# Attention queries written twice by GpSimd and turned once per head, in a two-layer diffusion trunk

## The chip, the cores and the metric

The kernel runs on one core of one Trainium2 chip. The metric is the device time of one execution in microseconds (us), the median of the runs. A core has TensorE (PE: matrix products and transposes; PEld is its weight load), VectorE (DVE), ScalarE (ACT), GpSimd (POOL) and SyncE (SP, which issues DMAs). Engines run side by side and wait for each other by semaphores. SBUF is the memory that all of them read; PSUM holds TensorE's results, in eight banks of 512 float32 per partition.

## The reference

Two trunk layers run over 1024 latent and 128 context tokens of width 1024. Each is modulated norm, mixer, then a mixture of experts. The change touches the attention of both mixers only. There, with queries and keys normalised and rotated:

```python
# layer 0: 8 query heads, 2 key/value heads, head width 64
s = jnp.einsum('bqkgd,bskd->bkgqs', qblk, k) * scale
pr = jax.nn.softmax(s, axis=-1)
return jnp.einsum('bkgqs,bskd->bqkgd', pr, v)

# layer 1: differential attention, 8 heads, two maps each, value width 128
s = jnp.einsum('bqphd,bsphd->bphqs', qblk, k) * scale
pr = jax.nn.softmax(s, axis=-1)
w = pr[:, 0] - lam * pr[:, 1]
return jnp.einsum('bhqs,bshe->bqhe', w, v)
```

All is float32. A float32 number x is used in TensorE's faster format as high part (x rounded to it) and low part (x less the high part), and a product is summed from the parts.

## The kernel before, in words

`attention` runs once per layer, in 2 groups of heads in layer 0 and 4 in layer 1; a group has 4 query maps (`nq`). In a group, the first part projects nine token tiles of 128 (`project`, t = 0 to 8), rotates and scales them on VectorE (`begin`, `finish_tile`) and leaves the queries in `qtok`. The second part runs over units (`unit_0`, `unit_1`). A unit is one query tile with one head: 4 units per tile in layer 0, 2 in layer 1, where a unit has two maps. One step of the unit loop issues, in TensorE's order, the scores of the next unit, transposes of the probabilities of an earlier one (`turn_probs`) and the product with the values of one still earlier (`values`).

Scores need the queries turned, with head width on the partitions. The contraction is 128 deep for a width of 64, since both halves of the partitions are used: the keys `ks` have their high part in one half and their low part in the other, and `qst` has for each map a first operand (v = 0) and a second (v = 1).

Before the change this is made so. For tile `qt`, VectorE (`split_queries`) writes the high part, the low part and the high part again into `qq`, three instructions of 128x256. TensorE (`stage_half`, L1271) turns it in two halves, each with four transposes of 128x128 into one bank; the windows [high, low] and [low, high] of `qq` give v = 0 and v = 1. ScalarE copies each bank into `qst` (L1398).

The order of the work is written out by hand: `program` and `unit_0`/`unit_1` are walked by TensorE and ScalarE, and VectorE has its own loop. All turns (keys, queries, probabilities) and the output of `values` share two PSUM banks in alternation. `next_bank` lets TensorE write a bank only when the reader of the use two places earlier is done: for a turn ScalarE's copy (`turn_read`), for an output VectorE's read (`o_read`). The scores use the other six banks, two sets of three in turn; VectorE takes their row maximum (`maxima`, L1691), ScalarE the exponential (L1467), and VectorE scales or mixes them (`mix`; L1703 in layer 0, L1709 in layer 1). L1310 are the transposes of the probabilities, L1327 and L1339 the products with the values.

GpSimd computes in this stage only inverse roots for the norms (L1150; in layer 1 L1154 and L1156 too).

## Time and profile before

| | us |
|---|---|
| median of 3 runs | 3293.04 (3290.2 to 3293.2) |
| span of the profiled execution | 3285.2 |
| PE, DVE, ACT, POOL busy in it | 3111.3, 2259.3, 1887.4, 618.3 |
| attention of layer 0, about | 225 to 595 |
| attention of layer 1, about | 1570 to 2358 |

The profile gives the span from the first to the last instruction; the run time of the profiled execution itself is not listed beside it. The median of the runs lies 7.8 us over the span. Part 2 of the page divides the span into 40 slices of 82 us, in tenths of busy time; attention is slices 3 to 7 and 20 to 28:

```profile
PE   6999989989999999997999999999997999999999
DVE  4777677557766666765686776867747666766666
PEclk9999999999999999998999999999998999999999
```

### The profile page before, as it was taken

How to read it: one execution, taken by the hardware profiler on the slowest of the kernel's cores; microseconds unless marked ns; L12 is line 12 of the kernel's file. 1: busy time of each engine (PE TensorE's matmuls, PEld its weight loads, DVE VectorE, ACT ScalarE, POOL GpSimd, SP SyncE). 2: the span in 40 equal slices, each digit the busy share in tenths (PEclk: the TensorE clock that was granted, in tenths of full speed). 3: DMA queues.
4: the chain of work that ended last, by engine and by line, in shares of the span. 5: the costliest groups of instructions: out<-in, count | busy, mean ns of one | idle time of the engine just before them, and what ended most of it. 6: DMA issues, size and time to landing. Idle time of an engine off the chain costs nothing. (4 is left out here: it accounts for less than half of the span.)

```text
span 3285.2 us, 55861 instructions
## 1 busy us (share of the span) xinstructions
PE 3111.3 (95%) x20268; PEld 2409.3 (73%) x20268; DVE 2259.3 (69%) x2853; ACT 1887.4 (57%) x2679; POOL 618.3 (19%) x479
## 2 busy tenths in 40 slices
PE   6999989989999999997999999999997999999999
PEld 4767878865777676765887888888885676767776
DVE  4777677557766666765686776867747666766666
ACT  3556848425665666554375583846723666556564
POOL 1200010001223322222111111021100222232221
PEclk9999999999999999998999999999998999999999
DMA  7230000449888888877010100100145888888885
GB/s 236 87 132 21 1 23 1 155 170 377 293 303 286 296 299 298 287 252 233 7 43 8 42 8 9 36 8 23 52 161 220 294 300 299 287 284 309 291 297 154
DMA packets 214175, 565.42 MB, mean 172 GB/s; under 512 B 33699, under 2 KB 71272, under 8 KB 213736
## 3 DMA queue, kind: packets, MB, share of 16 engines
q1 hardware_dynamic: 203614, 529.21, 44.6%
q0 software_dynamic: 9472, 33.57, 4.2%
q8 instruction: 111, 1.82, 0.2%
q14 instruction: 72, 0.59, 0.1%
q10 hardware_dynamic: 906, 0.23, 0.0%
HBM read 524.00 MB, written 38.94 MB: 171 GB/s over the span
## 5 line engine op out<-in xcount | busy, mean ns | idle before, releaser
L2188 DVE TENSOR_TENSOR moe_lo<-moe_raw,moeg_hi 128x2048 fp32r<-128x2048 f32 x384 | 882.8, 2327 | 289.3 <-ACT moeg_hi L2185 153.9
L2185 ACT CAST moeg_hi<-moe_raw 128x2048 fp32r<-128x2048 f32 x384 | 729.0, 1911 | 439.4 <-PE psum L2591 320.9
L1170 PE MATMUL psum<-attn_w_hi,attn_hs 128*128 128x512 f32 (+2 forms) x1424 | 368.3, 342 | 15.8 <-DVE attn_hs L1558 10.6
L1691 DVE TENSOR_REDUCE attn_neg_max<-psum 128x1 f32<-128x1280 f32 (+1 forms) x216 | 292.6, 1354 | 80.0 <-PE psum L1297 77.0
L1297 PE MATMUL psum<-attn_ks,attn_qst 128*128 128x512 f32 (+2 forms) x1200 | 310.7, 376 | 21.6 <-ACT attn_e L1467 19.5
L1467 ACT ACTIVATE attn_e<-psum,attn_neg_max 128x1280 f32<-128x1280 f32 (+1 forms) x216 | 264.6, 1226 | 60.9 <-DVE attn_neg_max L1691 54.8
L1170 PEld LDWEIGHTS psum<-attn_w_hi,attn_hs 128*128 128x128 f32 x1424 | 249.1, 189 | 47.8 <-DVE attn_hs L1558 11.8
L2591 PE MATMUL psum<-moe_lo,moeh_x_hi 128*128 128x512 f32 x960 | 262.0, 395 | 0.0
L2591 PE MATMUL psum<-moeg_hi,moeh_x_hi 128*128 128x512 f32 x960 | 261.6, 394 | 0.0
L2591 PE MATMUL psum<-moeg_hi,moeh_x_lo 128*128 128x512 f32 x960 | 260.6, 393 | 0.0
L1170 PE MATMUL psum<-attn_w_lo,attn_hs 128*128 128x256 f32 (+2 forms) x712 | 240.1, 337 | 0.0
L1297 PEld LDWEIGHTS psum<-attn_ks,attn_qst 128*128 128x128 f32 x1200 | 200.2, 190 | 51.3 <-ACT attn_e L1467 21.2
L2176 PE MATMUL psum<-moe_raw,moeh_xc 128*32 128x512 f32 x2048 | 236.2, 602 | 0.6 <-DMA moe_raw<-in_l_w_up 0.6
L2591 PEld LDWEIGHTS psum<-moeg_hi,moeh_x_hi 128*128 128x128 f32 x960 | 177.8, 188 | 51.1 <-issue 14.0
L1398 ACT COPY attn_pt<-psum 128x512 f32<-128x512 f32 (+2 forms) x400 | 191.7, 505 | 37.8 <-PE psum L1310 29.7
L2591 PEld LDWEIGHTS psum<-moeg_hi,moeh_x_lo 128*128 128x128 f32 x960 | 180.3, 188 | 42.1
L1310 PE MATMUL psum<-ident,attn_e 128*128 128x128 f32 x1296 | 197.4, 278 | 14.5 <-ACT attn_pt L1398 8.2
L2591 PEld LDWEIGHTS psum<-moe_lo,moeh_x_hi 128*128 128x128 f32 x960 | 180.5, 188 | 41.0
L1150 POOL TENSOR_TENSOR rstd<-ssq,neg_half 128x8 f32<-128x8 f32 (+1 forms) x54 | 80.0, 1482 | 548.6 <-DVE ssq L1590 548.6
L1310 PEld LDWEIGHTS psum<-ident,attn_e 128*128 128x128 f32 x1296 | 144.4, 141 | 48.0 <-issue 24.5
L2169 POOL COPY moeh_xc<-moe_x_ctx 128x64 f32 (+1 forms) x64 | 127.9, 2029 | 215.4 <-PE psum L2176 190.4
L1339 PE MATMUL psum<-attn_v,attn_pt 128*128 128x128 f32 x1296 | 158.3, 277 | 5.7 <-ACT attn_pt L1398 3.8
(360 smaller groups left out, 5389.7 us busy)
## 6 DMA issues: line engine op xcount, KB each, us to landing
moe_raw<-in_l_w_gate SPq DMA_DIRECT2D x256, 512.0 KB, 4.1
moe_raw<-in_l_w_up SPq DMA_DIRECT2D x256, 512.0 KB, 5.1
moe_raw<-in_l_w_down SPq DMA_DIRECT2D x128, 1024.0 KB, 6.1
ada_w<-in_l_ada_w SPq DMA_DIRECT2D x19, 1024.0 KB, 13.9
ada1h_w<-in_l_ada_w SPq DMA_DIRECT2D x9, 1024.0 KB, 10.7
lru_ada<-in_l_ada_w SPq DMA_DIRECT2D x8, 1024.0 KB, 7.7
lru_late<-in_l_ada_w SPq DMA_DIRECT2D x8, 1024.0 KB, 11.8
out_w<-in_l_w_out SPq DMA_DIRECT2D x16, 512.0 KB, 5.9
```

The costliest lines, as they stand in the source:

```text
L1170: last = pe.matmul(out, hs[t % 2][:, part, k, :], right, start=(i == 0 and n == 0), stop=(i == KB - 1 and n == 2))
L1297: last = pe.matmul(m.psum[:, into:into + step], qst[(u // per_tile) % 2][:, qm, v, :], ks[:, km, col:col + step], start=(v == 0), stop=(v ...
L1310: last = pe.transpose(m.psum[:, at + (i - b) * P:at + (i - b + 1) * P], src[:, i * P:(i + 1) * P], m.ident[:, :])
L1339: last = pe.matmul(m.psum[:, at:at + dv], pt[u % 2][:, i * P:(i + 1) * P], vt[:, kt, col:col + dv], start=(i == 0), stop=(i == len(tiles) ...
L1398: act.copy(out, src).then_inc(s["turn_read"], 1)
L1467: act.activation(out[:, 0:hi - lo], m.psum[:, score_at(n):score_at(n) + hi - lo], ACT.Exp, bias=neg_max[:, n:n + 1], accum_out=sums[:, n:n ...
L1691: dve.tensor_reduce(neg_max[:, n:n + 1], m.psum[:, score_at(n):score_at(n) + hi - lo], AX.X, ALU.max, negate=True).then_inc(s["maxed"], 1)
L2169: last = pool.tensor_copy(dst[:, :, j, :], mm.x_ctx[:, :, ds(e * 8 + j * P, 8)])
L2176: last = pe.matmul(m.psum[32 * g:32 * g + 32, 6 * BANK:7 * BANK], mm.xc[:, k, :], mm.raw[k][:, g // 2, (g % 2) * BANK:(g % 2 + 1) * BANK], ...
L2185: act.copy(mm.hi[slot % 4][:, :, :], mm.raw[slot][:, :, :]).then_inc(mm.s["hi_ready"], 1)
L2188: dve.tensor_tensor(mm.lo[slot][:, :, :], mm.raw[slot][:, :, :], mm.hi[slot % 4][:, :, :].bitcast(F32), ALU.subtract).then_inc(mm.s["lo_re ...
L2591: last = pe.matmul(m.psum[:, at:at + BANK], x[:, k, :], w[:, j, half * BANK:(half + 1) * BANK], start=(k == 0 and i == 0), stop=(k == KB - ...
```

## The change

GpSimd now writes each query tile twice over into `q_twice`, unsplit. TensorE turns it once per map, four transposes into one bank in place of eight into two, and the result lies on both halves of the partitions. ScalarE casts the bank into the first operand (high part, one copy of 128x512), and VectorE subtracts that from the bank to give the second operand (low part, 128x512). The bank is free after VectorE's subtraction (`q_low`).

```diff
+            def write_twice(j, qt):
+                wait_value(m, pool, s["k_split"], j * turns_k + (qt + PT_TILES + 1))
+                wait_value(m, pool, s["q_turned"], j * NT + qt)
+                view = qtok[:, qt, :].rearrange("p (n d) -> p n d", d=HD)
+                pool.tensor_copy(q_twice[:, :, :, :], view.unsqueeze(2).broadcast_to([P, nq, 2, HD])).then_inc(s["q_twice"], 1)
...
+                    if t in (3, 6):
+                        write_twice(j, (3, 6).index(t))
+                for u in range(units + OUT_LAG):
+                    if u % per_tile == 0 and u // per_tile + 2 < NT:
+                        write_twice(j, u // per_tile + 2)
+                    if l == 1 and u >= OUT_LAG:
+                        normal_of_out(j, u - OUT_LAG)
...
+                        elif what == "queries":
+                            pe.wait_ge(s["q_low"], j * NT + count)
...
-                def stage_half(qt, half):
...
+                def stage(qt):
+                    pe.wait_ge(s["q_twice"], j * NT + (qt + 1))
+                    at = next_bank(queries=qt)
+                    for i in range(nq):
+                        last = pe.transpose(m.psum[:, at + i * P:at + (i + 1) * P],
+                                            q_twice[:, i, :, :].rearrange("p v d -> p (v d)"), m.ident[:, :])
+                    last.then_inc(s["q_turned"], 1)
...
+                    act.wait_ge(s["q_turned"], j * NT + (qt + 1))
+                    act.copy(qst[qt % 2][:, 0, :, :], m.psum[:, at:at + nq * P].rearrange("p (n t) -> p n t", t=P)
+                             ).then_inc(s["q_high"], 1)
...
-                def split_queries(qt):
...
+                def subtract_high(qt):
+                    at = query_bank[qt]
+                    dve.wait_ge(s["q_high"], j * NT + (qt + 1))
+                    dve.tensor_tensor(qst[qt % 2][:, 1, :, :], m.psum[:, at:at + nq * P].rearrange("p (n t) -> p n t", t=P),
+                                      qst[qt % 2][:, 0, :, :].bitcast(F32), ALU.subtract).then_inc(s["q_low"], 1)
...
+    def stage_after(u):
+
+        qt = u // per_tile + (1, 2)[l]
+        return qt if u % per_tile == 1 and qt >= 2 and qt < NT else None
```

The orders also move. Tiles 2 to 8 are turned inside a unit step (`stage_after`): in layer 0 where both halves stood before, between the second and the third piece of the scores; in layer 1 in one odd step, where the halves stood in two steps. VectorE subtracts after the row maximum in layer 0, and after `mix` and before the second row maximum in layer 1. Tile 0's subtraction stands behind `project(4)`, tile 1's behind the first row maxima.

In the lists below, each name in `waits` is that of a semaphore's first use in the program; semaphores are used again under other names, and the text says which is meant. Lines after the change are L1284 (query turn), L1305 (scores), L1318 (turn of probabilities), L1347 (values), L1648 (subtraction), L1688 (row maximum).

TensorE in a step of layer 0 with a query turn, before:

```order
L1271 MATMUL psum<-ident,attn_qq 128x128 [waits ada0_8_row_read,ada0_8_turned]
L1271 MATMUL psum<-ident,attn_qq 128x128 x3
L1297 MATMUL psum<-attn_ks,attn_qst_2086 128x256 x2
L1271 MATMUL psum<-ident,attn_qq 128x128 [waits ada0_8_row_read]
L1271 MATMUL psum<-ident,attn_qq 128x128 x3
L1310 MATMUL psum<-ident,attn_e_2080 128x128 [waits ada0_8_row_read,lru_pad_zeroed]
L1310 MATMUL psum<-ident,attn_e_2080 128x128 x3
L1310 MATMUL psum<-ident,attn_e_2080 128x128 [waits ada0_8_row_read]
L1310 MATMUL psum<-ident,attn_e_2080 128x128 x3
L1297 MATMUL psum<-attn_ks,attn_qst_2086 128x512 [waits lru_gates_zeroed]
```

and now, where the last wait (printed `lru_gates_zeroed`) is for `q_low`:

```order
L1284 MATMUL psum<-ident,attn_q_twice 128x128 [waits ada0_8_row_read,ada0_8_turned]
L1284 MATMUL psum<-ident,attn_q_twice 128x128 x3
L1305 MATMUL psum<-attn_ks,attn_qst_2086 128x256 x2
L1318 MATMUL psum<-ident,attn_e_2080 128x128 [waits ada0_8_row_read,lru_h_split]
L1318 MATMUL psum<-ident,attn_e_2080 128x128 x3
L1318 MATMUL psum<-ident,attn_e_2080 128x128 [waits lru_gates_zeroed]
L1318 MATMUL psum<-ident,attn_e_2080 128x128 x3
L1305 MATMUL psum<-attn_ks,attn_qst_2086 128x512 [waits lru_h_high]
```

Four transposes and one bank are gone, and the second bank of the next turn of probabilities waits for VectorE in place of ScalarE.

VectorE around a query tile in layer 0, before:

```order
L1691 TENSOR_REDUCE attn_neg_max<-psum 128x1 [waits ada0_8_folded]
L1643 CAST attn_qq<-attn_qtok 128x4x64 [waits ada0_8_used]
L1644 CAST attn_qq<-attn_qtok 128x4x64
L1646 TENSOR_TENSOR attn_qq<-attn_qtok,attn_qq 128x4x64
L1691 TENSOR_REDUCE attn_neg_max<-psum 128x1 [waits ada0_8_folded]
L1698 RECIPROCAL attn_inv<-attn_sums 128x1 [waits lru_gates_zeroed]
L1703 TENSOR_SCALAR attn_e_2080<-attn_e_2080,attn_inv 128x1280
```

and now, from the reduction that reads the scores of the same step:

```order
L1688 TENSOR_REDUCE attn_neg_max<-psum 128x1 [waits lru_pad_zeroed]
L1648 TENSOR_TENSOR attn_qst_2085<-psum,attn_qst_2085 128x512 [waits lru_gates_loaded]
L1688 TENSOR_REDUCE attn_neg_max<-psum 128x1 [waits lru_pad_zeroed]
L1695 RECIPROCAL attn_inv<-attn_sums 128x1 [waits lru_h_high]
L1700 TENSOR_SCALAR attn_e_2079<-attn_e_2079,attn_inv 128x1280
```

The three small instructions are gone from another step, and the subtraction stands behind the row maximum.

TensorE in a step of layer 1 with (half) a query turn, before:

```order
L1271 MATMUL psum<-ident,attn_qq 128x128 [waits lru_gelu_square]
L1271 MATMUL psum<-ident,attn_qq 128x128 x3
L1297 MATMUL psum<-attn_ks,attn_qst_11285 128x512 x2
L1297 MATMUL psum<-attn_ks,attn_qst_11285 128x256 x2
L1215 REGISTER_ALU [waits o0_scored]
L1310 MATMUL psum<-ident,attn_e_11279 128x128 [waits lru_gelu_square]
L1310 MATMUL psum<-ident,attn_e_11279 128x128
L1215 REGISTER_ALU [waits lru_gelu_square]
L1339 MATMUL psum<-attn_v,attn_pt_11281 128x128 [waits lru_gelu_square]
L1339 MATMUL psum<-attn_v,attn_pt_11281 128x128 x9
```

and now, where L1347 waits (printed `lru_last_ready`) for `q_low`:

```order
L1284 MATMUL psum<-ident,attn_q_twice 128x128 [waits lru_gelu_square]
L1284 MATMUL psum<-ident,attn_q_twice 128x128 x3
L1305 MATMUL psum<-attn_ks,attn_qst_11173 128x512 x2
L1305 MATMUL psum<-attn_ks,attn_qst_11173 128x256 x2
L1231 REGISTER_ALU [waits o0_soft]
L1318 MATMUL psum<-ident,attn_e_11167 128x128 [waits lru_gelu_square]
L1318 MATMUL psum<-ident,attn_e_11167 128x128
L1322 MATMUL psum<-ident,attn_o_11191 128x128 [waits o0_parted]
L1347 MATMUL psum<-attn_v,attn_pt_11170 128x128 [waits lru_last_ready,lru_gelu_square]
L1347 MATMUL psum<-attn_v,attn_pt_11170 128x128 x9
```

The product with the values is the use two places behind the turn, and its bank now waits for VectorE.

VectorE in a step of layer 1, before:

```order
L1691 TENSOR_REDUCE attn_neg_max<-psum 128x1 [waits lru_gelu_tanh]
L1698 RECIPROCAL attn_inv<-attn_sums 128x2 [waits lru_last_ready]
L1705 TENSOR_SCALAR attn_ratio<-attn_sums,attn_inv,neg_lambda 128x1
L1709 SCALAR_TENSOR_TENSOR attn_e_11279<-attn_e_11280,attn_ratio,attn_e_11279 128x1280
L1690 REGISTER_ALU
L1691 TENSOR_REDUCE attn_neg_max<-psum 128x1 [waits lru_gelu_tanh]
L1641 REGISTER_ALU
L1643 CAST attn_qq<-attn_qtok 128x4x64 [waits lru_root_ready]
L1644 CAST attn_qq<-attn_qtok 128x4x64
L1646 TENSOR_TENSOR attn_qq<-attn_qtok,attn_qq 128x4x64
```

and now:

```order
L1688 TENSOR_REDUCE attn_neg_max<-psum 128x1 [waits o0_scored]
L1695 RECIPROCAL attn_inv<-attn_sums 128x2 [waits o0_expd]
L1702 TENSOR_SCALAR attn_ratio<-attn_sums,attn_inv,neg_lambda 128x1
L1706 SCALAR_TENSOR_TENSOR attn_e_11167<-attn_e_11168,attn_ratio,attn_e_11167 128x1280
L1648 TENSOR_TENSOR attn_qst_11173<-psum,attn_qst_11173 128x512 [waits lru_rec_done]
L1687 REGISTER_ALU
L1688 TENSOR_REDUCE attn_neg_max<-psum 128x1 [waits o0_scored]
```

The subtraction stands between the mix (L1706, before L1709) and the second row maximum.

## Rows read from the trace of the kernel before

**Rows 1.** Busy time in windows; window, length, busy (count) of each engine, PEclk, DMA.
```profile
225.00:270.00 45.00, 38.96 (x213) 35.90 (x214) 37.59 (x102) 15.96 (x36) 8.19 (x7) 1.00 0.02 4
...
300.00:400.00 100.00, 97.88 (x964) 82.18 (x964) 72.83 (x112) 80.53 (x142) 0.00 (x0) 1.00 0.01 1
...
1880.00:1930.00 50.00, 50.00 (x380) 46.19 (x380) 44.16 (x62) 44.83 (x99) 6.42 (x16) 1.00 0.00 1
```

**Rows 2.** Groups of instructions; count | busy us, mean ns | idle before.
```profile
L1271 PE MATMUL psum<-ident,attn_qq 128*128 128x128 f32 x432 | 65.3, 276 | 3.5 <-ACT attn_pt L1398 1.9 <-ACT attn_ks L1398 1.5
...
L1646 DVE TENSOR_TENSOR attn_qq<-attn_qtok,attn_qq 128x256 f32<-128x256 f32 x54 | 23.0, 425 | 5.1 <-issue 1.3
```

**Rows 3.** Windows of two units of layer 0, with and without a query turn.
```profile
309.87:318.31 8.44, 8.35 (x82) 7.00 (x80) 5.18 (x8) 6.91 (x13) 0.00 (x0) 1.00 0.00 0
318.31:325.55 7.24, 7.24 (x75) 6.15 (x73) 6.00 (x11) 5.68 (x11) 0.00 (x0) 1.00 0.01 2
```

**Rows 4.** Timeline of layer 0; start us, us, engine, instruction, [idle before <-releaser].
```profile
312.06 0.60 PE L1271 MATMUL psum<-ident,attn_qq 128*128 128x128 f32 x4
...
312.42 0.49 PE L1297 MATMUL psum<-attn_ks,attn_qst 128*128 128x256 f32 x2
...
312.70 1.26 ACT L1398 CAST attn_qst<-psum 128x512 fp32r<-128x512 f32 x2 [0.53 <-PE psum L1271]
...
312.94 1.49 DVE L1691 TENSOR_REDUCE attn_neg_max<-psum 128x1 f32<-128x1280 f32 x1 [1.20 <-PE psum L1297]
...
313.43 1.24 PE L1310 MATMUL psum<-ident,attn_e 128*128 128x128 f32 x8
...
314.43 0.71 PE L1297 MATMUL psum<-attn_ks,attn_qst 128*128 128x512 f32 x2
```

**Rows 5.** Timeline of layer 0 near 280 us, VectorE to TensorE.
```profile
279.83 0.89 DVE L1703 TENSOR_SCALAR attn_e<-attn_e,attn_inv 128x1280 f32<-128x1280 f32 x1
...
280.78 1.09 PE L1310 MATMUL psum<-ident,attn_e 128*128 128x128 f32 x8 [0.19 <-DVE attn_e L1703]
```

**Rows 6.** Single lines; count: duration ns min/median/max, first and last start, shapes.
```profile
L1600 DVE TENSOR_TENSOR attn_zb<-psum,attnw_sin x64: 410/414/416, 1575.6 to 2235.5; 128x256 f32<-128x256 f32 x64
...
L2783 DVE TENSOR_TENSOR moeh_hid_lo<-psum,moeh_hid_hi x30: 1223/1224/1225, 821.0 to 3225.0; 128x1024 fp32r<-128x1024 f32 x30
...
L2481 POOL CAST moeh_x_hi<-moeh_x_tmp x30: 1041/1041/1496, 791.9 to 3207.4; 128x1024 fp32r<-128x1024 f32 x30
...
L2169 POOL COPY moeh_xc<-moe_x_ctx x64: 233/2295/2332, 766.5 to 3182.8; 128x64 f32 x48, 128x64 f32<-128x64 f32 x16
```

**Rows 7.** Timeline of layer 1, from 1888 us.
```profile
1888.75 1.04 PE L1310 MATMUL psum<-ident,attn_e 128*128 128x128 f32 x8
...
1890.09 0.60 PE L1271 MATMUL psum<-ident,attn_qq 128*128 128x128 f32 x4
...
1890.45 0.95 PE L1297 MATMUL psum<-attn_ks,attn_qst 128*128 128x512 f32 x4
...
1890.94 1.55 DVE L1709 SCALAR_TENSOR_TENSOR attn_e<-attn_e,attn_ratio,attn_e 128x1280 f32<-128x1280 f32 x1
...
1891.56 2.40 PE L1339 MATMUL psum<-attn_v,attn_pt 128*128 128x128 f32 x20
...
1892.41 1.48 DVE L1691 TENSOR_REDUCE attn_neg_max<-psum 128x1 f32<-128x1280 f32 x1
...
1894.95 1.17 PE L1310 MATMUL psum<-ident,attn_e 128*128 128x128 f32 x8
```

**Rows 8.** Timeline of layer 1, opening of a group.
```profile
1859.10 0.73 PE L1297 MATMUL psum<-attn_ks,attn_qst 128*128 128x512 f32 x2 [1.15 <-ACT attn_e L1467]
```

**Rows 9.** Timeline of an experts' stage: GpSimd and VectorE.
```profile
987.00 2.38 POOL L2483 TENSOR_TENSOR moeh_x_lo<-moeh_x_tmp,moeh_x_hi 128x1024 fp32r<-128x1024 f32 x1 [0.32 <-issue]
...
988.88 4.85 DVE L2188 TENSOR_TENSOR moe_lo<-moe_raw,moeg_hi 128x2048 fp32r<-128x2048 f32 x2 [3.31 <-PE psum L2176]
...
996.06 4.48 DVE L2188 TENSOR_TENSOR moe_lo<-moe_raw,moeg_hi 128x2048 fp32r<-128x2048 f32 x2
```

More of the change, by code:

```diff
@@ L937, in attention @@
     qst_at = put.pos[0]
-    qst = [put(f"qst{i}", [P, nq, 2, P], F32R) for i in range(2)]
-    qq = put("qq", [P, nq, 3, HD])
+    qst = [put(f"qst{i}", [P, 2, nq, P], F32R) for i in range(2)]
+    q_twice = put("q_twice", [P, nq, 2, HD])
+    put("spare", [P, nq, HD])
     khl_at = put.pos[0]
@@ L1022, in unit_1 @@
             make["scores"](u + 1, 1, 0)
-        if half_after(u) is not None:
-            make["stage_half"](*half_after(u))
+        if stage_after(u) is not None:
+            make["stage"](stage_after(u))
         if u >= 1:
@@ L1200, in group, with next_bank @@
                 turn, uses, keys_at = [0], [], {}
-                def next_bank(output=None, last=None):
+                def next_bank(output=None, last=None, queries=None):
                     n = len(uses)
@@ L1217, in next_bank @@
                         uses.append(("last", last))
+                    elif queries is not None:
+                        uses.append(("queries", queries + 1))
                     else:
@@ L1260, in last_v @@
                     pe.sem_inc(s["w_used"], 1)
-                staged = {}
-                def stage_half(qt, half):
-                    if half == 0:
-                        pe.wait_ge(s["q_split"], j * NT + (qt + 1))
-                    at = next_turn()
-                    for i in range(2):
-                        flat = qq[:, 2 * half + i, :, :].rearrange("p v d -> p (v d)")
-                        for v in range(2):
-                            last = pe.transpose(m.psum[:, at + (2 * i + v) * P:at + (2 * i + v + 1) * P],
-                                                flat[:, v * HD:v * HD + P], m.ident[:, :])
-                    last.then_inc(s["turned"], 1)
-                    staged[qt, half] = turn[0]
-                def stage(qt):
-                    for half in range(2):
-                        stage_half(qt, half)
+                def stage(qt):
+                    pe.wait_ge(s["q_twice"], j * NT + (qt + 1))
[4 more added lines that the diff above has]
+                    last.then_inc(s["q_turned"], 1)
                 def scores(u, which, piece=None):
@@ L1283, in scores @@
                     if piece in (None, 0):
-                        if u % per_tile == 0:
-                            pe.wait_ge(s["turn_read"], j * TURNS + staged[u // per_tile, (1, which)[l]])
+                        if u % per_tile == 0 and which == 0:
+                            pe.wait_ge(s["q_low"], j * NT + (u // per_tile + 1))
                         if u == 0 and which == 0:
@@ L1663, in count_last, with count_stage @@
                         used[0] += 1
-                def count_half(qt, half):
-                    count[0] += 1
+                def count_stage(qt):
+                    query_bank[qt] = turn_bank(used[0])
                     used[0] += 1
-                    staged_at[qt] = count[0]
-                def count_stage(qt):
-                    for half in range(2):
-                        count_half(qt, half)
                 def count_probs(u, part):
@@ L1683, in group @@
                 program(dict(cache_keys=count_cache, project=none, last_z=count_last, last_v=count_last, turn_keys=count_keys,
-                             stage=count_stage, stage_half=count_half, scores=none, exps=none, turn_probs=count_probs, values=count_values, ahead=none), last_group)
+                             stage=count_stage, scores=none, exps=none, turn_probs=count_probs, values=count_values, ahead=none), last_group)
                 def maxima(u, which):
```

66 lines of the change are left out of this document (25 added, 41 removed).

## The prediction

> **What bounds the kernel now.** I read the busy time in windows first, because the change touches only the attention stages. The reader is to see that the kernel has two kinds of stretch there [rows 1]. In the projection of layer 0 (225 to 270 us) TensorE is busy 38.96 of 45 us and VectorE 37.59, so VectorE sets the pace. In the unit loops TensorE is busy 97.88 of 100 us in layer 0 and all of 50.00 us in layer 1. There, an instruction taken off TensorE shortens the kernel, and any new wait of TensorE lengthens it. VectorE is at 73% in the unit loop of layer 0 and at 88% in that of layer 1, so it isn't the bound, but it works in order, and what stands in its queue ahead of a signal decides when the signal comes.
>
> Second, the groups of instructions: TensorE turns queries 432 times, 65.3 us busy, and VectorE's subtraction for them runs 54 times at 425 ns [rows 2]; 54 is 9 tiles times 6 groups. Third, the timelines of one step of each layer, which carry the sum.
>
> **TensorE's saving.** 216 of the 432 transposes go. Four of them occupy TensorE for 0.36 us when they flow: the query turn starts at 1890.09 and the next product at 1890.45 [rows 7]. The 0.60 us of the row holds the tail of the pipeline, which overlaps. In layer 0 the turn costs more: a pair of units with it takes 8.44 us and one without it 7.24 [rows 3], so 1.20 for eight transposes, of which 0.72 is work and 0.48 waits for ScalarE's casts of the two banks.
>
> **The new wait.** Before, the bank of a query turn was free when ScalarE had copied it. Now it is free when VectorE has subtracted, and VectorE comes to that only after what stands before it in its own list. In both layers TensorE wants that bank again two uses later. The orders of the instructions say which instruction that is: in layer 0 the second bank of the next turn of probabilities, in layer 1 the product with the values. Behind it stands everything else of TensorE, and so the next scores, their maxima and exponentials.
>
> Layer 0, tiles 2 to 8. The third piece of the scores is issued at 312.42, and the row maximum starts after it at 312.94, after 1.20 us of idleness, and takes 1.49 [rows 4]. Neither changes, since four transposes still stand ahead of that piece. VectorE starts an instruction some 0.08 us before the one ahead ends (mix from 1890.94 for 1.55, next at 1892.41) [rows 7]. So the subtraction starts at 314.35; ScalarE's cast, which starts at 312.70 [rows 4], is over long before. Its duration isn't in the trace in this shape. The nearest rows are a product with a PSUM operand of 128x256 at 0.41 and a subtraction from PSUM of 128x1024 at 1.22 [rows 6]; between them by width, 128x512 takes 0.68, which I use, with 0.41 and 1.22 as ends. TensorE starts 0.06 after a signal of VectorE (279.83 + 0.89 = 280.72, start 280.78) [rows 5]. That gives 314.35 + 0.68 + 0.06 = 315.09, and 0.36 for the four transposes: 315.45 for the next scores, which start at 314.43 now [rows 4]. Net +1.02 us per tile, the saved transposes included. There are 7 tiles in 2 groups: 14 x 1.02 = +14.3 us. Nothing takes it back, as TensorE has next to no idle time in the loop.
>
> Layer 1, tiles 2 to 8. In the odd step four transposes remain, so nothing is saved there. The mix runs from 1890.94, the next place in VectorE's list is at 1892.41, and there the subtraction goes: it ends at 1893.09, TensorE goes on at 1893.15. It wants to start the values at 1891.56 [rows 7]. Stall 1.59 us. In the even step the other half goes, 0.36, and with VectorE's three small instructions gone the turn of probabilities takes 1.04 in place of 1.17, since it waited there for the output's read behind them [rows 7]: 0.13 more. Net 1.59 - 0.36 - 0.13 = +1.10 us per tile. Tiles 3 to 8 in 4 groups: 24 x 1.10 = +26.4 us. The second row maximum comes 0.6 later in VectorE's list, but its scores' exponential isn't wanted before TensorE's next step, which is itself 1.59 later.
>
> Tile 1 and 2 of layer 1 are staged in the opening of the unit loop, where TensorE waits for exponentials (1.15 us at 1859.10) [rows 8], so VectorE's order counts directly: two subtractions of 0.68 come in, and three small instructions, at most 3 x 0.425 = 1.28 [rows 2], go. That is between 0 and 0.7; I take 0.4, 4 x 0.4 = +1.6 us. Tile 0 of layer 1 is turned while TensorE sets the pace: -0.36 x 4 = -1.4 us. Tiles 0 and 1 in layer 0: VectorE loses its small instructions and gets a subtraction, in its own stretch; within 0.6 us per group either way, taken as nothing.
>
> **GpSimd and ScalarE.** GpSimd is idle in the unit loop of layer 0 and busy 6.42 of 50 us in that of layer 1 [rows 1]. It now makes 54 copies of 128x512. A cast of 128x1024 takes 1.04 and a copy of 128x64 0.23 at best [rows 6]; by width between them 0.6. Each copy starts when the tile before has been turned and is wanted two to four steps later, some 12 us in layer 1 and 16 in layer 0, so even 2.38, the slowest row of 128x1024 [rows 9], costs TensorE nothing. ScalarE has one cast less per tile; in the unit loop it is off the path, worth nothing. The clock: TensorE was granted 1.00 (2.4 GHz) also in the stretch where it was 87% busy [rows 1], so I charge nothing for stalls of 1.6 us.
>
> **The sum.** 14.3 + 26.4 + 1.6 - 1.4 = +40.9 us on the span of 3285.2, so 3326.1; the median of the runs lies 7.8 above the span, so 3293.04 + 40.9 = 3334. If the subtraction took 0.41, 42 tiles would give 11 less; at 1.22, 23 more.
>
> **Rival 1, the bank is free in time (faster).** If VectorE's subtraction were done before TensorE wants the bank, only the saving would stand: layer 0 14 x (1.20 - 0.36) = 11.8, layer 1 28 x 0.49 = 13.7, tile 0 1.4, together -27: 3266 us. It decides at 1891.56 in layer 1. In layer 0 the turn of probabilities starts at 313.43 [rows 4] and would start up to 0.7 earlier (0.36 of work, the rest waits), its second bank 0.36 later: between 313.1 and 313.8. For it: VectorE is idle 1.20 us ahead of the row maximum in layer 0. Against it: its list has the maximum first, and that waits for a later product.
>
> **Rival 2, GpSimd holds VectorE up.** The trace shows that the two exclude each other: a 128x64 copy takes 0.23 at best and 2.30 in the median [rows 6], and where GpSimd's subtraction runs until 989.38, VectorE's two from 988.88 take 4.85 in place of 4.48 [rows 9]. If each copy in layer 1 met the mix and held it for 0.6, the stall would grow by that: 28 x 0.6 = 17, so 3351. Against it: in layer 1 the copy stands behind GpSimd's roots, after the mix, while VectorE reads PSUM. In layer 0 the scaling isn't on the way to the bank.
>
> The Trainium skill, page "SBUF — State Buffer", section "SBUF: two separate sides", says the same more sharply: GpSimd and a VectorE instruction with two SBUF inputs or in a two-port mode share one pair of ports, and whichever starts first keeps it for the whole instruction. The 4.85 us agree. By that rule a subtraction with one operand in PSUM would not be blocked, the mix would.
>
> **Rival 3, half of the stall is made up.** While TensorE waits, VectorE and ScalarE catch up, and small waits behind go. Layer 0 has 2.1 us of TensorE's idle time in 100 [rows 1], layer 1 none, so it would need turns of probabilities that wait without being seen. Half of the sum: +20, 3313.
>
> **How the numbers follow.** Forecast 0.74, with a range of its own of 3322 to 3350; rival 2 0.10; rival 3 0.08; rival 1 0.06; that it all cancels 0.02. The range of 8 in 10 goes from 3314 to 3353: below by the short subtraction and part of rival 3, above by rival 2 and a longer subtraction. A difference of 0.2% (6.6 us) is about what can be told from none. Faster 0.06, same 0.02, slower 0.92.
>
> **What would show it.** In the profile after: L1318 in layer 0 and L1347 in layer 1 idle ahead of them for 1.3 to 2.0 and for 1.6 us, released by L1648, 14 and some 24 to 28 times, together near 65 us; a pair of units with a turn in layer 0 at 9.5 us; two units of layer 1 at 13.5 in place of 12.4 (2 x 6.2, from 1888.75 to 1894.95 [rows 7]); L1648 at 0.68 us; GpSimd's copy at 0.6. The prediction is wrong if those waits are not there, if VectorE subtracts before the maximum ends, or if the mix (L1706) is longer than 1.55 or starts late with GpSimd busy.

## The result, and the profile after

| | before | after |
|---|---|---|
| median of 4 runs, us | 3291.62 | 3349.51 |
| lowest to highest, us | 3289.72 to 3293.2 | 3347.78 to 3350.99 |
| profiled execution: time, us | not listed | 3347.78 |
| profiled execution: span, us | 3285.2 | 3345.8 |
| granted clock of the profiled execution, mean | 0.988 | 0.982 |

The ratio is 1.0174, with a 95% interval of 1.016 to 1.0189. The kernel became 57.9 us slower; 40.9 were forecast, with a range of 3314 to 3353 that holds the result. The span grew by 60.6 us. The profiled execution of the kernel before is one of its shorter ones: its spans on record beside the experiments go from 3285.2 to 3297.2 us. So what is read from the two traces lies some 3 us above the loss of the medians.

Windows of the changed kernel, as [rows 1]: window, length, busy time (count) of TensorE matmuls, weight loads, VectorE, ScalarE and GpSimd, then the granted clock. The first lies in layer 0's unit loop, the second in layer 1's. The third is the opening of the unit loop of layer 1's second group, where the granted clock is 0.56.

```profile
300.00:400.00 100.00, 90.40 (x888) 76.35 (x888) 66.41 (x93) 72.82 (x128) 3.08 (x5) 1.00 0.01 1
1910.00:1960.00 50.00, 45.30 (x328) 40.28 (x327) 40.46 (x48) 39.11 (x87) 7.27 (x19) 1.00 0.00 1
...
1885.00:1892.00 7.00, 5.98 (x25) 4.97 (x24) 6.15 (x8) 3.76 (x6) 0.62 (x1) 0.56 1.03 296
```

TensorE, which was busy 97.88 of 100 us and all of 50, now stands idle for 9.6% and 9.4% of the first two. That is most of the loss; VectorE and ScalarE became less busy too, so neither is the new bound.

Whom TensorE waits for, in layer 0's stage, then in layer 1's; columns: us in total, times, the longest.

```profile
PE psum L1318 <- DVE attn_qst L1648: 24.4, 14, 1.7
PE psum L1184 <- DVE attn_hs L1565: 7.4, 10, 1.0
```

```profile
PE psum L1347 <- DVE attn_qst L1648: 35.6, 24, 3.6
PE psum L1305 <- ACT attn_e L1474: 15.1, 13, 2.6
```

L1648 is VectorE's subtraction. The two lines foretold, L1318 (the second bank of the next turned probabilities) and L1347 (the values), wait for it 14 and 24 times, 60 us together. L1339, which is L1347 in the kernel before, waited for VectorE 1.7 us in all of layer 1 before.

The timeline of one step of layer 0, the answer to [rows 4]: start us, us, engine, instruction, idle time before it and what ended it.

```profile
314.49 0.60 PE L1284 MATMUL psum<-ident,attn_q_twice 128*128 128x128 f32 x4
314.85 0.49 PE L1305 MATMUL psum<-attn_ks,attn_qst 128*128 128x256 f32 x2
315.13 0.59 ACT L1461 CAST attn_qst<-psum 128x512 fp32r<-128x512 f32 x1 [0.53 <-PE psum L1284]
315.17 0.60 PE L1318 MATMUL psum<-ident,attn_e 128*128 128x128 f32 x4
...
315.37 1.49 DVE L1688 TENSOR_REDUCE attn_neg_max<-psum 128x1 f32<-128x1280 f32 x1 [1.20 <-PE psum L1305]
...
316.78 0.68 DVE L1648 TENSOR_TENSOR attn_qst<-psum,attn_qst 128x512 fp32r<-128x512 f32 x1
317.52 0.66 PE L1318 MATMUL psum<-ident,attn_e 128*128 128x128 f32 x4 [1.75 <-DVE attn_qst L1648]
317.93 0.71 PE L1305 MATMUL psum<-attn_ks,attn_qst 128*128 128x512 f32 x2
```

It reads as the working had it: the maximum, then the subtraction, then 0.06 us, then TensorE, which had been ready for 1.75 us. ScalarE's cast was over at 315.72, a microsecond before VectorE came to it.

One odd step of layer 1, the answer to [rows 7]:

```profile
1913.01 1.33 ACT L1474 ACTIVATE attn_e<-psum,attn_neg_max 128x1280 f32<-128x1280 f32 x1 [0.87 <-DVE attn_neg_max L1688]
1913.60 1.03 PE L1318 MATMUL psum<-ident,attn_e 128*128 128x128 f32 x8
...
1914.48 0.73 PE L1305 MATMUL psum<-attn_ks,attn_qst 128*128 128x512 f32 x2
1914.62 1.06 ACT L1406 COPY attn_pt<-psum 128x512 f32<-128x512 f32 x2
...
1915.25 0.66 PE L1284 MATMUL psum<-ident,attn_q_twice 128*128 128x128 f32 x4
...
1915.79 1.55 DVE L1706 SCALAR_TENSOR_TENSOR attn_e<-attn_e,attn_ratio,attn_e 128x1280 f32<-128x1280 f32 x1
...
1917.26 0.68 DVE L1648 TENSOR_TENSOR attn_qst<-psum,attn_qst 128x512 fp32r<-128x512 f32 x1
1917.86 1.48 DVE L1688 TENSOR_REDUCE attn_neg_max<-psum 128x1 f32<-128x1280 f32 x1
1918.09 2.13 PE L1347 MATMUL psum<-attn_v,attn_pt 128*128 128x128 f32 x17 [1.15 <-DVE attn_qst L1648]
```

The values start 2.84 us after the turn of the queries; before, 1.47 (1890.09 to 1891.56). The pieces of the two kernels in windows of two units, as [rows 3]: layer 0 with a query turn, without, and layer 1.

```profile
312.29:321.82 9.53, 7.79 (x79) 6.61 (x77) 5.79 (x9) 6.37 (x12) 0.62 (x1) 1.00 0.00 0
321.82:329.05 7.23, 7.23 (x74) 6.13 (x72) 5.19 (x8) 5.67 (x11) 0.00 (x0) 1.00 0.01 2
1913.60:1927.31 13.71, 12.53 (x92) 11.19 (x91) 10.78 (x13) 10.61 (x24) 2.05 (x5) 1.00 0.01 1
```

Layer 0: 9.53 (9.5 foretold) against 8.44, and 7.23 unchanged. Layer 1: 13.71 against 12.54, taken from the first eight turns of probabilities to the same turns two units on. The 12.54 is a longer pair than most: from one query turn to the next but one, the pairs behind it take 12.42 (1896.42 to 1908.84).

Where along the program the 60 us came, by the starts of the 216 exponentials in both traces: layer 0's two groups +15.8; the four unit loops of layer 1 +11.2, +10.3, +11.0 and +7.4; between them +4.3.

One row doesn't fit the forecast, the step of layer 1 in which tile 8's queries are turned. L1565 is VectorE's subtraction for the first tokens of the next group (their split into high and low part):

```profile
1756.98 1.23 DVE L1565 TENSOR_TENSOR attn_hs<-region,attn_hs 128x1024 fp32r<-128x1024 f32 x1 [2.45 <-ACT attn_hs L1387]
...
1761.92 0.68 DVE L1648 TENSOR_TENSOR attn_qst<-psum,attn_qst 128x512 fp32r<-128x512 f32 x1
...
1762.75 4.10 PE L1347 MATMUL psum<-attn_v,attn_pt 128*128 128x128 f32 x20 [3.58 <-DVE attn_qst L1648]
```

There the values wait 3.58 us and then take 4.10 in place of 2.40. The granted clock, 1.00 in all of that stretch before, is 0.5 there, which is 1.2 GHz. In windows of 2.5 us over the two stages (225 to 640 and 1570 to 2440), stretches at 0.5 sum up to 41 us after and 3.5 before.

Where these stretches lie matters for the argument. There are ten, and none of them comes behind one of the steady waits of 1.1 to 1.8 us. Two follow tile 8's wait of 3.58. Two follow a wait between the unit loops of two groups, before the next projection (L1184), and three a wait for exponentials in an opening of layer 1. One wait of each of the last two kinds, after the change and then before it:

```profile
1801.00 0.79 PE L1184 MATMUL psum<-attn_w_hi,attn_hs 128*128 128x512 f32 x1 [3.15 <-issue]
1884.46 1.42 PE L1305 MATMUL psum<-attn_ks,attn_qst 128*128 128x512 f32 x6 [2.35 <-ACT attn_e L1474]
```

```profile
1772.65 0.49 PE L1170 MATMUL psum<-attn_w_hi,attn_hs 128*128 128x512 f32 x1 [1.74 <-issue]
1855.65 1.43 PE L1297 MATMUL psum<-attn_ks,attn_qst 128*128 128x512 f32 x6 [1.74 <-ACT attn_e L1467]
```

Both waits grew, and in the kernel before no stretch at 0.5 follows them. The other three stretches lie in layer 0: two behind a wait of 2.71 us in its openings, which the kernel before has too with the clock at 1.00, and one at its end, as before. What TensorE waits for at L1184 the profile doesn't show.

### The profile page after: what moved, and what is told of

It is laid out like the page before. It is cut to its first block and busy times, and to the rows that moved or that the text cites. A ratio compares the mean times of both kernels' runs of the same rounds, so it can differ in the third digit from the quotient of the medians.

```text
span 3345.8 us, 55316 instructions
## 1 busy us (share of the span) xinstructions
PE 3107.4 (93%) x20052; PEld 2401.7 (72%) x20052; DVE 2247.6 (67%) x2745; ACT 1859.4 (56%) x2625; POOL 654.0 (20%) x533
## 5 line engine op out<-in xcount | busy, mean ns | idle before, releaser
L1184 PE MATMUL psum<-attn_w_hi,attn_hs 128*128 128x512 f32 (+2 forms) x1424 | 371.7, 344 | 18.8 <-DVE attn_hs L1565 10.6
L1688 DVE TENSOR_REDUCE attn_neg_max<-psum 128x1 f32<-128x1280 f32 (+1 forms) x216 | 292.2, 1354 | 110.1 <-PE psum L1305 108.7
L1305 PE MATMUL psum<-attn_ks,attn_qst 128*128 128x512 f32 (+2 forms) x1200 | 308.8, 379 | 20.4 <-ACT attn_e L1474 18.0
L1184 PEld LDWEIGHTS psum<-attn_w_hi,attn_hs 128*128 128x128 f32 x1424 | 251.0, 190 | 52.6 <-DVE attn_hs L1565 12.8
L1305 PEld LDWEIGHTS psum<-attn_ks,attn_qst 128*128 128x128 f32 x1200 | 205.6, 192 | 54.6 <-ACT attn_e L1474 20.4
L1184 PE MATMUL psum<-attn_w_lo,attn_hs 128*128 128x256 f32 (+2 forms) x712 | 241.4, 339 | 0.0
L1318 PE MATMUL psum<-ident,attn_e 128*128 128x128 f32 x1296 | 201.1, 281 | 36.8 <-DVE attn_qst L1648 26.1
L2589 PEld LDWEIGHTS psum<-moe_lo,moeh_x_hi 128*128 128x128 f32 x960 | 180.4, 188 | 41.1
L1347 PE MATMUL psum<-attn_v,attn_pt 128*128 128x128 f32 x1296 | 162.7, 281 | 41.2 <-DVE attn_qst L1648 35.6
L1318 PEld LDWEIGHTS psum<-ident,attn_e 128*128 128x128 f32 x1296 | 148.7, 143 | 67.9 <-DVE attn_qst L1648 27.7
L1347 PEld LDWEIGHTS psum<-attn_v,attn_pt 128*128 128x128 f32 x1296 | 153.1, 195 | 49.7 <-issue 33.0
```

What stands on the lines that cost most here:

```text
L1184: last = pe.matmul(out, hs[t % 2][:, part, k, :], right, start=(i == 0 and n == 0), stop=(i == KB - 1 and n == 2))
L1305: last = pe.matmul(m.psum[:, into:into + step], qst[(u // per_tile) % 2][:, v, qm, :], ks[:, km, col:col + step], start=(v == 0), stop=(v ...
L1318: last = pe.transpose(m.psum[:, at + (i - b) * P:at + (i - b + 1) * P], src[:, i * P:(i + 1) * P], m.ident[:, :])
L1347: last = pe.matmul(m.psum[:, at:at + dv], pt[u % 2][:, i * P:(i + 1) * P], vt[:, kt, col:col + dv], start=(i == 0), stop=(i == len(tiles) ...
L1688: dve.tensor_reduce(neg_max[:, n:n + 1], m.psum[:, score_at(n):score_at(n) + hi - lo], AX.X, ALU.max, negate=True).then_inc(s["maxed"], 1)
L2589: last = pe.matmul(m.psum[:, at:at + BANK], x[:, k, :], w[:, j, half * BANK:(half + 1) * BANK], start=(k == 0 and i == 0), stop=(k == KB - ...
```

## The experiments

Each was run beside the kernel before on the same chip; "against before" is the difference of the medians, and "the change" is the changed kernel, +57.9.

| | median, us | against before | ratio, 95% interval |
|---|---|---|---|
| e1_late_both | 3317.66 | +23.4 | 1.0061 to 1.0088 |
| e2_late_l0 | 3321.18 | +26.9 | 1.0071 to 1.0102 |
| e3_late_l1 | 3345.21 | +50.9 | 1.0146 to 1.0178 |
| e4_filled | 3376.24 | +81.9 | 1.0233 to 1.0264 |
| e5_pool_split | 3278.78 | -14.2 | 0.9938 to 0.9965 |
| e6_sub_first | 3305.36 | +12.4 | 1.0027 to 1.0057 |
| e7_tokens_later | 3342.54 | +49.6 | 1.0133 to 1.0164 |
| e8_narrow_low | 3334.06 | +41.1 | 1.0106 to 1.0137 |
| e9_pool_fill | 3276.61 | -13.1 | 0.9946 to 0.9973 |
| e10_pool_double | 3298.89 | +9.2 | 1.0017 to 1.0038 |
| e11_small_copy | 3350.75 | +61.0 | 1.0166 to 1.0197 |
| e12_pool_fill_later | 3278.14 | -11.6 | 0.9952 to 0.998 |

**The place of the turn (e1, e2, e3).** The edit in TensorE's and ScalarE's order, where EARLY names the layers:

```diff
@@ unit_0
-        if stage_after(u) is not None:
+        if 0 not in EARLY and stage_after(u) is not None:
...
                 make["exps"](n, 0)
+                if 0 in EARLY and n == u and stage_after(u) is not None:
+                    make["stage"](stage_after(u))
@@ unit_1
-        if stage_after(u) is not None:
+        if 1 not in EARLY and stage_after(u) is not None:
...
             make["turn_probs"](u - lag, 1)
+        if 1 in EARLY and stage_after(u) is not None:
+            make["stage"](stage_after(u))
```

VectorE's subtraction moves too: in layer 0 ahead of the scaling, in layer 1 behind the second row maximum.

e1_late_both: 

> The query turn is moved, for tiles from 2 on, to the last place before the values are multiplied: in layer 0 it stands in the even step, after all products and turns of that step but the values, in layer 1 in the odd step behind the four turns of probabilities; VectorE subtracts right behind the row maximum that it would do there anyway. Nothing is left out. Theory (the loss is the wait for the bank, 42 times, 61.8 us on L1318 and L1347 together in the trace after): the bank is wanted again only after a stretch of 2.4 us of values in which VectorE subtracts, so these waits go and the saving of the transposes stands: 20 to 27 us faster than before, 3265 to 3272. Rival (the loss comes from TensorE's lower granted clock, GpSimd's copies or VectorE's and ScalarE's work as such): the time stays within 15 us of the change's 3349. If the moved subtraction delays the mix in layer 0 by 0.7 us and that is wanted at once, some 10 us are lost of the gain: 3275 to 3285.

e2_late_l0: 

> The same move in layer 0 alone; layer 1 as in the change. Theory: the 14 waits of 1.7 to 2.0 us on L1318 go, and with them the 15.8 us that layer 0 lost by the exponentials' start times; the saving of 0.84 us for each of 14 tiles comes out: 26 us less than the change, 3323. Rival (layer 0's loss is not the wait but the turn's place beside ScalarE's casts): less than 10 us less than the change, above 3339.

e3_late_l1: 

> The same move in layer 1 alone; layer 0 as in the change. Theory: 24 waits on L1347 (35.6 us) go; layer 1 lost about 44 us by the exponentials' start times, of which the waits explain 36 and the rest is taken to follow from them (late exponentials, a lower granted clock for some 25 us): so all of it goes and a saving of 0.36 to 0.49 us for each of 24 tiles comes on top: 3349 less 44 to 56, so 3293 to 3305. Rival A (what the waits don't explain has its own cause): 3349 less 36, 3313, or more. Rival B (layer 1's loss is GpSimd or ScalarE): above 3335. Layers are independent: the gains of the two partial moves against the change should add up to that of the move in both within 5 us.

Layer 0 came out as expected (3321 for 3323): its waits for the subtraction fell from 14 to none, and each tile takes 0.84 us less than before the change. Layer 1 did not, 3345 for 3293 to 3305, and so e1 missed too (3318 for 3265 to 3272). The trace of e3 says why. Whom TensorE waits for in layer 1 of e3, and the step (L1352 is the product with the values, L1653 the subtraction, L1411 ScalarE's copy of turned probabilities):

```profile
PE psum L1352 <- ACT attn_pt L1411: 44.9, 29, 3.6
```

```profile
1910.11 0.38 PE L1323 MATMUL psum<-ident,attn_e 128*128 128x128 f32 x2
...
1910.43 0.60 PE L1289 MATMUL psum<-ident,attn_q_twice 128*128 128x128 f32 x4
...
1912.15 0.36 ACT L1411 COPY attn_pt<-psum 128x256 f32<-128x256 f32 x1
...
1912.57 2.50 PE L1352 MATMUL psum<-attn_v,attn_pt 128*128 128x128 f32 x20 [1.53 <-ACT attn_pt L1411]
```

Two banks take turns. With the query turn between them, the values now want the bank of the probabilities turned at 1910.11, and ScalarE reads that bank only at 1912.15, behind an exponential. VectorE's late reader was exchanged for ScalarE's late reader, at nearly the same price: e3 is 7 us faster than the change. The expectation had looked at the bank of the queries and not at whose bank the values would inherit.

**The place of the subtraction (e6).** On top of e2:

```diff
+                    if l == 1 and stage_after(u) is not None:
+                        subtract_high(stage_after(u))
                     if l == 1 and u < units:
                         mix(u)
```

> The late query turn in layer 0 (3321.2 measured alone) and, in layer 1, the turn at its place but VectorE's subtraction ahead of the mix of the same step instead of behind it. Nothing is left out. Theory (the place in VectorE's list sets when the bank comes free): the subtraction then waits for ScalarE's cast only (over at 1916.92 in the step where it now starts at 1917.64), so the values start 0.6 to 0.8 us earlier in 24 steps, and the mix and the second row maximum end 0.7 to 1.4 later, which has cover until the exponential's bank is wanted: 3301 to 3308. Rival (the mix or the maximum has no such cover; its lateness costs as much as the bank's wait gains): 3315 to 3330.

3305, as the theory had it: 14.5 us less than e2, with nothing changed but VectorE's order. The wait for the subtraction fell to 13.6 us in 24 times, and a part came back elsewhere: TensorE waits for exponentials (whose maximum is now later) 28.5 us in 40 times, against 16.6 in 13 in e2.

**The length of the subtraction (e8).**

```diff
+                    if qt >= 2:
+                        dve.tensor_tensor(qst[qt % 2][:, 1, 0, 0:64], m.psum[:, at:at + 64],
+                                          qst[qt % 2][:, 0, 0, 0:64].bitcast(F32), ALU.subtract).then_inc(s["q_low"], 1)
+                        return
```

> The changed kernel, but for tiles from 2 on VectorE's subtraction is only 128x64 of its 128x512: 7/8 of the low parts are left out. Theory (each of 38 to 42 waits ends when this instruction ends): with 0.2 to 0.3 us in place of 0.68 the waits are 0.4 to 0.48 shorter each, 15 to 20 us: 3329 to 3334; a little more if the stretches at a granted clock of 0.5 go too. Rival (the wait's end is set by something else, such as ScalarE's cast or GpSimd): within 5 us of 3349.

16.8 us less than the change. The short subtraction takes 0.216, so 0.47 less, in 42 tiles 19.6: some 85% of what VectorE saves there reaches the end.

**GpSimd's copies (e11).**

```diff
+                if qt >= 2:
+                    pool.tensor_copy(q_twice[:, 0, 0, 0:8], view[:, 0, 0:8]).then_inc(s["q_twice"], 1)
+                    return
```

> The changed kernel, but for tiles from 2 on GpSimd copies only 128x8 of the queries' 128x512: the rest of them is left out. Theory (the copies are hidden): within 4 us of the changed kernel's 3349.5. Rival (GpSimd's copies hold VectorE's mix up or come late for the turn): 5 to 17 us faster.

3 us more than the change (+61.0 against +57.9), where the rival would be 5 to 17 faster. The copies are hidden.

**The step with the tokens (e7).**

```diff
-                {12: [TOKENS], 15: [2], 16: [0, 4], 17: [1, 7], 18: [3], 19: [5, 6]}][l]
+                {14: [TOKENS], 15: [2], 16: [0, 4], 17: [1, 7], 18: [3], 19: [5, 6]}][l]
```

> The changed kernel, but in layer 1 the split of the next group's first tokens (ScalarE's cast, VectorE's subtraction 128x1024) is asked for two units later (14 instead of 12), away from the step in which tile 8's queries are turned. Nothing is left out. In the changed kernel the values of that step start 3.58 us late in three of four groups, and they and the next products then take place at a granted clock of 0.5. Theory (the two stand in one chain through VectorE, and the long wait brings the clock down): the 3.58 becomes 1.2 as in the other steps and the three stretches at 0.5 go: 3 x 3 to 3 x 4 us, so 3338 to 3341. Rival (the stretches at 0.5 come from something else, or the split costs the same wherever it stands): 3346 to 3352.

8.3 us less than the change, a little short of the theory: the longest wait for the subtraction fell from 3.6 to 1.5 us. The stretches at 0.5 did not go: those behind tile 8's wait did, others appeared, in sum 40 us for 41, and the mean granted clock over the runs stayed at 0.982. So the tokens' split made the long wait, but taking the long wait away did not bring the clock back.

**The wait filled (e4).**

```diff
                 def next_turn():
+                    fill = len(uses) > 30 and uses[-1][0] == "queries"
                     at = next_bank()
+                    if fill:
+                        spare_products(m, pe, (14, 12)[l], at // BANK)
```

> The changed kernel with spare products (their result is thrown away) issued on TensorE behind each query turn of tiles from 2 on, before the turn of probabilities that follows: 14 of them in layer 0, 12 in layer 1, so that TensorE works through most of the wait for VectorE's subtraction. Nothing is left out. Theory of the clock (the trace after shows the granted clock at 0.5, which is 1.2 GHz, in about 11 short stretches of the two loops, some 37 us together, where the trace before has none): with the wait filled the clock stays at 1.00 there and up to 13 us come back, 3336 to 3345. Rival (the dips have another cause, or the spare products cost more than the wait): no change, or slower by what overshoots: 3349 to 3365, with dips still there.

The condition fills 12 of layer 0's 14 steps and 20 of layer 1's 28. Slower by 24 us than the change, so the forecast of a gain was wrong: 12 spare products took 2.84 us, more than twice the 1.15 that they were to fill, and TensorE's surplus went onto the path. The mean granted clock over the runs rose, from 0.9818 to 0.9848, but the trace (the execution at 0.983) doesn't tie that to the filled waits: the two stages still hold 41 us at 0.5, in openings and between the loops, where nothing was filled.

**The bank freed by ScalarE (e5, e9, e10, e12).** ScalarE copies, GpSimd splits:

```diff
+            def split_turned(j, qt):
+                wait_value(m, pool, s["q_high"], j * NT + (qt + 1))
+                turned = q_twice.rearrange("p n v d -> p n (v d)")
+                pool.tensor_copy(qst[qt % 2][:, 0, :, :], turned)
+                pool.drain()
+                pool.tensor_tensor(qst[qt % 2][:, 1, :, :], turned, qst[qt % 2][:, 0, :, :].bitcast(F32), ALU.subtract).then_inc(s["q_low"], 1)
+                pool.drain()
@@ next_bank
-                            pe.wait_ge(s["q_low"], j * NT + count)
+                            pe.wait_ge(s["q_high"], j * NT + count)
@@ ScalarE, stage
-                    act.copy(qst[qt % 2][:, 0, :, :], m.psum[:, at:at + nq * P].rearrange("p (n t) -> p n t", t=P)
-                             ).then_inc(s["q_high"], 1)
+                    act.copy(q_twice.rearrange("p n v d -> p (n v d)"), m.psum[:, at:at + nq * P]).then_inc(s["q_high"], 1)
```

> The changed kernel, the query turn at its place in both layers, but the bank is freed by ScalarE alone: it copies the turned queries as they are (128x512, 0.6 us) into SBUF, and GpSimd makes the high part (cast) and the low part (subtraction) from that copy; VectorE does nothing for queries. Nothing is left out. Theory (what costs is that the bank's last reader stands late in its engine's list; the rest of the loss follows from these waits): ScalarE's copy is over within 1 us of the turn, so no wait is left on the bank and the saving of the transposes stands: 3262 to 3275, that is 20 to 30 us faster than before. Rival 1 (the moved place in the bank order or ScalarE's list is itself late, as in the move behind the turns of probabilities, where the values waited 1.5 us for ScalarE instead): above 3300. Rival 2 (GpSimd holds VectorE's mix up, since cast and subtraction read and write SBUF for some 2 to 3 us per tile): the mix in layer 1 shows up longer than 1.55 us, and the time lies 10 to 40 us above the theory's.

3278.8: faster than the change by 72 us and than the kernel before by 14 (the ratio gives 16), though not by the 20 to 30 expected. Its step of layer 1 (L1297 the query turn, L1419 ScalarE's copies, L1360 the values):

```profile
1891.46 0.73 PE L1318 MATMUL psum<-attn_ks,attn_qst 128*128 128x512 f32 x2
1891.60 1.06 ACT L1419 COPY attn_pt<-psum 128x512 f32<-128x512 f32 x2
...
1892.23 0.66 PE L1297 MATMUL psum<-ident,attn_q_twice 128*128 128x128 f32 x4
...
1893.76 1.50 PE L1360 MATMUL psum<-attn_v,attn_pt 128*128 128x128 f32 x12
```

The values follow the query turn after 1.53 us and wait for no one. But the queries start at 1892.23, 0.77 after the scores ahead of them (0.55 before the change): their bank is that of the first turned probabilities, which ScalarE copies from 1891.60. So layer 1's steady tiles gain 0 to 0.2 us each and not 0.49, its unit loops 6 us in sum; layer 0's tiles gain 0.68 each.

e9 fills each opening of layer 1 with spare products, e10 does each query turn twice, e12 is e9 with the tokens' split of e7:

```diff
@@ e9, e12: scores
+                    if l == 1 and u == 2 and which == 0:
+                        at = next_bank()
+                        uses.pop()
+                        spare_products(m, pe, 8, at // BANK)
@@ e10: stage
-                    for i in range(nq):
+                    for i in (*range(nq), *range(nq)):
```

e9_pool_fill: 

> The split by GpSimd (3278.8 measured alone) with 8 spare products on TensorE in each opening of layer 1's unit loop, just ahead of the third unit's scores, where TensorE stands idle for 2.28 us. Nothing is left out. In that kernel no wait on the query turn's bank is left, yet about 30 us of the two attention stages ran at a granted clock of 0.5 (before: 3.5 us), one piece of it right behind such an opening, where six products took 2.09 us in place of 1.43. Theory (what that kernel lacks against the 3266 of the free bank is the clock: the saved transposes make TensorE's idle stretches longer): with the openings filled the stretches at 0.5 in the openings go, 2 of 9, and 2 to 5 us come back: 3273 to 3277. Rival (the missing 12 us have another cause): 3277 to 3281, with or without the stretches.

e10_pool_double: 

> The split by GpSimd, but every query turn does its four transposes twice, into the same bank: TensorE's work is again that of 432 transposes. Nothing is left out. Theory (the gain of that kernel is TensorE's 0.36 us for each turn): 54 x 0.36 = 19 us slower where each counts, less what the openings hide (8 of 54), so +16: 3295; if the fuller TensorE brings the granted clock back to that of before, up to 13 less: 3282. Rival (the gain came from ScalarE's or VectorE's relief): within 4 us of 3279 with the clock unchanged.

e12_pool_fill_later: 

> The split by GpSimd with the filled openings and the split of the next group's first tokens asked for at unit 14 in place of 12. Nothing is left out. In the changed kernel that move alone gave 7 us, since there a wait of 3.6 us for VectorE became 1.2; here the values wait for no one of VectorE's list. Theory: the move gives nothing or 1 to 2 us here, so within 2 us of the filled openings alone: 3272 to 3278. Rival (the step with the tokens' split costs by VectorE's and ScalarE's lists themselves): 4 to 7 us faster than the filled openings alone, 3267 to 3271.

e9 can't be told from e5 (3276.6, ratio 0.9959 against 0.9952), so what the filled openings are worth stays open; in its trace the openings' long wait fell from 2.3 to 0.5 us with the clock at 1.00 there, yet that wait was for the exponentials, and only its clock could be won. e10 is 22 to 23 us slower than e9 and e5: 54 turns of four transposes at 0.41 to 0.43. So in e5 TensorE's saved transposes are worth their time, at a bit more than 0.36 for each turn, and the rival (ScalarE's or VectorE's relief) is out. e12 gains nothing over e9: where the values don't wait for VectorE, the tokens' split costs nothing. That is the theory's side, at 3278.

The best of all is e5 or e9, 0.4 to 0.5% faster than before.

## Why the prediction was right, and where not

**The mechanism holds.** The bank of the query turn waits for an instruction that stands late in VectorE's list. It is shown by its waits (38 at the two places foretold), by its removal in layer 0 (e2, -31 us against the change), by the subtraction's order (e6, -14.5), its length (e8, -16.8), and by the reader exchanged (e5, -72).

**L1648 at 0.68 us, GpSimd's copy at 0.6.** Measured 0.683 and 0.616 in the median. Both estimates by width held.

**Layer 0, +14.3.** Measured +15.8 at the exponentials, 1.06 per steady tile for 1.02.

**Layer 1, steady tiles, 24 x 1.10 = +26.4: mis-sized.** Measured +38.0 over the 24 tiles that this term spans. Tiles 3 to 7 cost 1.13 to 1.59 each, 1.30 in the mean, and tile 8 cost 4.1, 2.4, 4.1 and 1.3 us in the four groups.

First, the steady tiles. The stall came out as the working had it. From the scores ahead of the query turn to the values TensorE takes 3.61 us (1914.48 to 1918.09), for 2.02 before (1889.54 to 1891.56):

```profile
1889.54 0.71 PE L1297 MATMUL psum<-attn_ks,attn_qst 128*128 128x512 f32 x2
```

That is 1.59 more, the size forecast. What was too large is the saving of 0.49. Its second part, 0.13, was read from one turn of probabilities of 1.17; the turns in the next two steps (1901.29 and 1907.50) took 1.04 before the change already. The half turn that is gone gave 0.46: from the scores to the next turn of probabilities 1.24 us (1922.35 to 1923.59) for 1.70 (1902.08 to 1903.78). And 0.17 was lost anew: the scores behind the delayed values come 2.22 after them for 2.15, and the scores at 1928.20 come 0.89 behind the turn of probabilities for 0.79, as ScalarE's exponential ends only at 1928.06. 1.59 - 0.46 + 0.17 is the 1.30. So the stall and the saving were not independent. In the last group, where nothing is prepared for a next one, most tiles cost 1.13 to 1.15, close to the forecast.

Second, tile 8: there the next group's tokens are split on ScalarE and VectorE in the same step, and the prediction, which read one step, took it for all. In the two groups with 4.1 the values run at 0.5 behind the wait; in the group with 2.4 the wait is as long and the clock stays at 1.00. The e7 kernel, with the split moved away, is 8.3 us faster than the change.

**"So I charge nothing for stalls of 1.6 us": a term put at nothing.** It rested on one stretch, 87% busy and at 1.00. For the steady stalls it held in this trace: both loop windows of 100 and 50 us are at 1.00. It failed for the clock as a whole: the stretches at 0.5 come behind longer waits, at tile 8, in openings and between the loops, which the prediction did not have. That these waits bring the low clock is not shown. The mean granted clock was 0.986 over 31 runs of the kernel before, and 0.982 over 4 of the change. A mean lower by 0.0043 over 3347 us is 14 us of full-speed time, the most that it can cost; by the 31 runs of before, whose span goes from 3286 us at 0.988 to 3297 at 0.983, so 2.2 us for each 0.001, it is about 9. Forecast plus clock is 50 to 55, for 57.9 measured. The 3 to 8 us that are left are of the size by which tile 8's step exceeds the others in three groups (7 us), but part of those 7 is the clock's, so the two can't be added cleanly. What lowers the clock is not settled: e4 fills the steady stalls and keeps 41 us at 0.5, e7 took 6 us of waiting away without a change of the clock, e5 has none of these stalls and still runs at 0.984, with 28 us at 0.5 in the two stages, two stretches of it (at 1957 and 2155) behind waits of no more than 1.14 us.

**Openings, +1.6, and tile 0, -1.4.** Openings cost 0 to 1.3 us each by the exponentials, 2.0 in sum. Tile 0's saving isn't seen: between the unit loops +4.3 came, 5.7 more than foretold. The first two of the three transitions took +1.8 and +3.4, each with the wait of 3.15 us and a stretch at 0.5 behind it.

**Rivals.** Rival 1 is excluded by the waits. A bank that is free in time is possible, but not with this order of VectorE's list; e5 shows the case, at -14 instead of -27, since layer 1 gave 6 us there and not 13.7. Rival 2 gives the right time, 3351, for a wrong reason: the mix (L1706) never took more than 1.554 us, and with 42 of the 54 copies cut to 128x8 nothing is gained (e11). A time in agreement was no evidence here. Rival 3, that half is made up, is out; waits came on top.

## What to carry to other kernels

When two banks take turns, list for every use who reads it last, where that reader stands in its engine's order, and which use two places on inherits the bank; a move of one use shifts all inheritances, and it only helps if the heir's reader is early. Give the freeing of a shared bank to the engine that gets there first, and let a slower engine work on the copy. Read each kind of step before multiplying one, above all the step in which something else is prepared; and where a forecast adds idle time to TensorE, put a lower granted clock into the range.

## What the runs showed of the hardware

The granted clock differs between runs of one kernel, and the span with it: e5's five runs had means from 0.983 to 0.985 and spans from 3279.9 to 3273.2 us.

GpSimd and VectorE's mix do hold each other up, where GpSimd subtracts in SBUF. In the opening of a group in e5 (L1159 is GpSimd's subtraction, L1714 the mix, L1151 its copy):

```profile
1850.46 1.26 POOL L1159 TENSOR_TENSOR attn_qst<-attn_q_twice,attn_qst 128x512 fp32r<-128x512 f32 x1
...
1851.29 1.78 DVE L1714 SCALAR_TENSOR_TENSOR attn_e<-attn_e,attn_ratio,attn_e 128x1280 f32<-128x1280 f32 x1
...
1852.12 1.42 POOL L1151 COPY attn_q_twice<-attn_qtok 128x512 f32<-128x512 f32 x1 [0.40 <-issue]
```

The mix, 1.55 elsewhere, takes 1.78 when it starts inside GpSimd's subtraction, and the copy, 0.61 in most tiles, takes 1.42 when it starts inside the mix: it ends 0.47 after the mix does. That was so in each of the four groups (1.76 to 1.94 for the mix). The Trainium skill, page "SBUF — State Buffer", section "SBUF: two separate sides", calls the shared ports an exclusive lock, held for the whole instruction by whoever starts first; the trace agrees for the copy within 0.14 us, while the mix lost 0.23 us of the 0.43 that it overlapped. The prediction's "the 4.85 us agree" has the same gap: VectorE lost 0.37 there of an overlap of 0.50 ([rows 9]). Spans on GpSimd are rough in this profile.
